# The chunk products of an RWKV-7 recurrence: 96 for 128, with operands laid side by side and over both partition halves

## The chip, the core and the metric

The kernel runs on one core of a Trainium2 chip. The metric is the device time of one execution in microseconds (us). Before the change it is 1353.78 us, the median of three runs from 1351.94 to 1355.68 us. All values are fp32.

## What is computed

One decoder layer over 1024 tokens of width 1024. A projection feeds two groups of heads, RWKV-7 (8 heads of 64) and latent attention (8 heads); their outputs are projected, added and normalised, and a feed-forward net of width 4096 follows. The change lies in the RWKV-7 recurrence, which the reference states token by token, for each head with a 64 x 64 state S:

```python
def step(S, inp):
    r_t, w_t, k_t, v_t, kk_t, a_t = inp
    sa = einsum('bhvk,bhk->bhv', S, -kk_t)
    S = S * w_t + sa (x) (kk_t * a_t) + v_t (x) k_t      # (x): outer product
    y = einsum('bhvk,bhk->bhv', S, r_t)
```

## The kernel before, in words

The recurrence (`rwkv_chunks`, L1603 to L1978) doesn't go token by token. It takes 16 chunks of 64 tokens, and in each chunk does the work of all eight heads with matrix products of 64 x 64. Heads are laid out as four tiles (`RT` = 4, loop variable c) of 128 partitions, and each tile holds two heads, one on partitions 0 to 63 and one on 64 to 127 (loop variable p, `own[p]`). A product of one head is so one matmul with 64 rows and 64 columns of TensorE, and the two heads of a tile stand at different places of the array. In the trace each fp32 matmul is two LDWEIGHTS and two MATMUL instructions; a tile shape such as 64*128 is rows * columns of the stationary operand in the array. "A pair" below is two MATMUL instructions, one for p = 0 and one for p = 1, that run side by side; the fp32 matmuls of both heads of a tile are two pairs.

PE's order is written out by hand in `stage(m, ...)` (L1803). Stage m does the chain of chunk n = m - 1 and prepares chunk m:

- `first_product(m)` (L1798): `low_t` times `inv`, 8 matmuls into bank `B_T1`
- `rhs_step(n)` (L1697): 16 matmuls, masked key scores times values, plus `kk` times state
- `scores_step(m)` (L1749): 24 matmuls. Three products of one form, decayed key with `kk` (A), decayed key with decayed receptance (R), and beta with decayed receptance
- `sa_step(n)` (L1713): 8 matmuls, the solve, into `B_SA`; ScalarE copies it to `u` (L1853)
- `product(B_X, ...)` (L1819): 8 matmuls, the second half of the chunk inverse; VectorE merges it (L1914)
- `transposes(m)` (L1767): 24 matmuls. Beta, decayed key and values, each times an identity or the centring matrix
- `state_step(n)` (L1722): 16 matmuls, two terms summed, key tokens times values and beta tokens times `u`
- `y_step(n)` (L1735): 24 matmuls, three terms summed

That makes 128 matmuls, or 256 MATMUL instructions, in a stage. Stages 1 to 15 do both halves; stage 16 has the chain alone, and before stage 1 chunk 0 is prepared.

ScalarE goes in the fixed order `product_out` (L1847), two exponentials (L1840, L1841), `u_step`, `tokens_step` (L1863 values, L1864 beta and key), `y_leave` (L1857). VectorE goes `rhs_out` (L1900), `mask_step` (L1923, L1925), `merged` (L1914), `state_out` (L1904, L1908), `r_step` (L1893). GpSimd makes the decayed key (L1977). SyncE's queue loads three 64 x 64 operands a head for chunk m, six DMAs (L1685), and for m >= 3 first waits for the solve of chunk m - 3 (L1678).

Of the kernel before, what the change touches and what calls it, by code (L numbers as in the profile page):

```python
# [24 lines left out]
P = 128  # L25
# [9 lines left out]
RT = RW // P  # L35
# [1567 lines left out]
def rwkv_chunks(nc, mem, k):  # L1603
# [26 lines left out]
    kd = [k.first_kd, new("k_undecayed", tile)]  # L1630
    rd = [k.first_rd] + new("r_decayed", tile, copies=2)
    ks = new("k_scores", [P, RT, 2, CH], copies=2)
    bs = new("b_scores", tile, copies=2)
    inv_t, inv, low_t = ([first] + new(name, tile, copies=2)
                         for first, name in zip(k.first_tiles, ("inverse_t", "inverse", "low_t")))
    bk_tok = new("bk_tok", [P, 2, RT, CH], copies=2)
    v_tok = new("v_tok", tile, copies=2)
    u = new("u", tile)
# [9 lines left out]
    B, K, A_, R = 0, 1, 0, 1  # L1648
    B_SA, B_RY, B_T1, B_X, B_KS, B_B, B_BKT, B_V = range(8)
    Y0 = RT  # L1650
    cols = lambda c: slice(c * CH, (c + 1) * CH)
    view = lambda bank, n=RT, at=0: ps[:, bank, at * CH:(at + n) * CH].rearrange("p (c n) -> p c n", n=CH)
    now = lambda m: slice(m * CH, (m + 1) * CH)

    with ExitStack() as ctx:
        exps, kd_ready, rd_ready, scores_mm, tr_done, sc_ready, tok_ready = sems(
            nc, ctx, "d_exps", "d_kd_ready", "d_rd_ready", "d_scores_mm", "d_tr_done", "d_sc_ready", "d_tok_ready")
# [11 lines left out]
        def _(sp):  # L1669
# [6 lines left out]
            for m in range(1, NC_):  # L1676
# [6 lines left out]
                for x, dst in ((k.inv_t_d, inv_t), (k.inv_d, inv), (k.low_d, low_t)):  # L1683
                    for p in range(2):
                        sp.dma_start(dst[m % 3][own[p], :, :], matrices(x)[:, m, p].rearrange("c r j -> r c j"))\  # L1685
                            .then_inc(base_in[m % 3], 16)
            sp.wait_ge(gate_in, 16)
# [6 lines left out]
        def _(pe):  # L1694
            mm = nc.tensor.matmul

            def rhs_step(n):  # L1697
                q, a = n % 2, n % 3
                pe.wait_ge(sc_ready, n + 1)
                pe.wait_ge(v_ready, n + 1)  # L1700
# [3 lines left out]
                for c in range(RT):  # L1704
                    for p in range(2):
                        mm(ps[own[p], B_RY, cols(c)], ks[q][own[p], c, A_, :], v_tok[q][own[p], c, :],
                           start=True, stop=False)
# [5 lines left out]
            def sa_step(n):  # L1713
                pe.wait_ge(rhs_ready, n + 1)
                pe.wait_ge(xt_up, n + 1)
                for c in range(RT):
                    for p in range(2):
                        last = mm(ps[own[p], B_SA, cols(c)], inv_t[n % 3][own[p], c, :], rhs[own[p], c, :],
                                  start=True, stop=True)
                last.then_inc(sa_mm, 1)  # L1720

            def state_step(n):  # L1722
                q = n % 2
                pe.wait_ge(tok_ready, n + 1)
                pe.wait_ge(sa_ready, n + 1)
                for c in range(RT):
                    for p in range(2):
                        mm(ps[own[p], B_SA, cols(c)], bk_tok[q][own[p], K, c, :], v_tok[q][own[p], c, :],
                           start=True, stop=False)
                    for p in range(2):  # L1730
                        last = mm(ps[own[p], B_SA, cols(c)], bk_tok[q][own[p], B, c, :], u[own[p], c, :],
                                  start=False, stop=True)
                last.then_inc(s_mm, 1)

            def y_step(n):  # L1735
                q, a = n % 2, n % 3
                for c in range(RT):
# [11 lines left out]
            def scores_step(m):  # L1749
                q, a = m % 2, m % 3  # L1750
                if m >= 1:
                    pe.wait_ge(kd_ready, m)
                    pe.wait_ge(rd_ready, m)
                    pe.wait_ge(sc_ready, m)
                for c in range(RT):
                    for p in range(2):
                        mm(ps[own[p], B_KS, cols(2 * c + A_)], kd[q][own[p], c, :], kk_all[own[p], c, now(m)],
                           start=True, stop=True)
                    for p in range(2):
                        mm(ps[own[p], B_KS, cols(2 * c + R)], kd[q][own[p], c, :], rd[a][own[p], c, :],  # L1760
                           start=True, stop=True)
                    for p in range(2):
                        last = mm(ps[own[p], B_B, cols(c)], beta[own[p], c, now(m)], rd[a][own[p], c, :],
                                  start=True, stop=True)
                last.then_inc(scores_mm, 1)

            def transposes(m):  # L1767
# [6 lines left out]
                for c in range(RT):  # L1774
                    for p in range(2):
                        mm(ps[own[p], B_BKT, cols(B * RT + c)], beta[own[p], c, now(m)], k.eye[own[p], :],
                           start=True, stop=True)
                    for p in range(2):
                        mm(ps[own[p], B_BKT, cols(K * RT + c)], kd[q][own[p], c, :], k.eye[own[p], :],
                           start=True, stop=True)  # L1780
                if m == 0:
                    pe.wait_ge(centred, 1)
                if m == 1 or m and m % 4 == 0:
                    pe.wait_ge(v_in[m // 4], 16)
                for c in range(RT):
                    for p in range(2):
                        v = hT[own[p], T_V + c, now(m)] if m else k.first_v[own[p], c, :]
                        last = mm(ps[own[p], B_V, cols(c)], v, centre[own[p], :], start=True, stop=True)
# [9 lines left out]
            def first_product(m):  # L1798
                z = m % 3
                pe.wait_ge(base_in[z], 96 * (m // 3 + (z > 0)))  # L1800
                product(B_T1, low_t[z], inv[z]).then_inc(t1_mm, 1)

            def stage(m, chain, ahead):  # L1803
# [11 lines left out]
                if ahead:  # L1815
# [3 lines left out]
                    product(B_X, prod, inv_t[z]).then_inc(xt_mm, 1)  # L1819
# [6 lines left out]
            product(B_T1, low_t[0], inv[0]).then_inc(t1_mm, 1)  # L1826
# [6 lines left out]
        def _(act):  # L1833
# [9 lines left out]
            def product_out(n):  # L1843
# [3 lines left out]
                A(prod[:], view(B_T1), ACT.Copy).then_inc(t1_out, 1)  # L1847

            def u_step(n):
                act.wait_ge(sa_mm, n + 1)  # L1850
                if n >= 1:
                    act.wait_ge(y_mm, n)
                A(u[:], view(B_SA), ACT.Copy).then_inc(sa_ready, 1)  # L1853
# [5 lines left out]
            def tokens_step(m):  # L1859
# [3 lines left out]
                A(v_tok[m % 2][:], view(B_V), ACT.Copy).then_inc(v_ready, 1)  # L1863
# [1378 lines left out]
```

## Time and profile before

| | |
|---|---|
| median of three runs | 1353.78 us |
| profiled execution, own time | 1353.33 us |
| its span | 1351.5 us |
| PE (TensorE) busy | 1315.0 us, 97% |
| VectorE busy | 945.5 us, 70% |
| ScalarE busy | 474.8 us, 35% |
| GpSimd busy | 497.0 us, 37% |
| TensorE clock granted | 0.998 of full speed (mean) |
| recurrence | from 475 to 605 us of the span, about a tenth |

A busy PE is not PE at its peak: matmuls are pipelined and overlap in the records, so what the recurrence costs is read from the times between the starts of instructions and not from their durations.

### The profile page before, as it was taken

What the parts mean: (1) busy time and instruction counts of PE and PEld (TensorE: products, weight loads), DVE (VectorE), ACT (ScalarE), POOL (GpSimd) and SP (SyncE); (2) the same over time, 40 slices, a digit from 0 to 9 for tenths busy, and PEclk for the clock granted to TensorE, in tenths of its full rate; (3) what the DMA queues carried; (4) which work ended last, traced back from release to release, by engine and by line L of the source; (5) the groups of instructions that cost most, each with busy time, mean ns of one, the idle gap of its engine ahead of it and who ended that gap; (6) DMA issues with size and microseconds to landing.
All of it is one profiled execution on the core that took longest, in us unless ns stands there. A gap on an engine that the chain in (4) does not pass through costs nothing.

```text
span 1351.5 us, 23894 instructions
## 1 busy us (share of the span) xinstructions
PE 1315.0 (97%) x9900; PEld 1071.2 (79%) x9900; DVE 945.5 (70%) x1110; ACT 474.8 (35%) x796; POOL 497.0 (37%) x323
## 2 busy tenths in 40 slices
PE   7999999999999989989999999999999999999997
PEld 6877677877776789986688878888888888888886
DVE  3657975257777634439677988877777787669877
ACT  3143643146555433334104522212222444333330
POOL 0000112001876210002084778766774354444030
PEclk9999999999999999999999999999999999999999
DMA  5111444779639952224222345444436986666562
GB/s 225 62 48 32 141 157 156 184 169 292 183 101 288 221 127 53 59 64 140 87 101 94 117 137 198 142 147 164 156 125 226 356 288 219 190 198 200 190 205 106
DMA packets 147372, 214.50 MB, mean 159 GB/s; under 512 B 79960, under 2 KB 86240, under 8 KB 146624
## 3 DMA queue, kind: packets, MB, share of 16 engines
q1 hardware_dynamic: 146976, 211.92, 49.3%
q8 instruction: 79, 1.29, 0.4%
q10 hardware_dynamic: 288, 1.05, 0.2%
q14 instruction: 29, 0.24, 0.1%
HBM read 137.89 MB, written 66.39 MB: 151 GB/s over the span
## 4 chain that ended last, share of the span: by engine, by line
PE 49%; DVE 3%; POOL 1%; issue 1%; ACT 1%; DVEq 0%; POOLq 0%; ACTq 0%
PE banks L2523 23%; PE banks L2410 18%; PE banks L2326 5%; PE banks L2398 2%; POOL tile_h L3083 1%; PE banks L2371 1%; DVE wout_lo L2736 0%; POOL tile_s L3083 0%; DVE y_all L2756 0%; DVE first_relu L2870 0%; PE banks L2352 0%; DVE gn_scale L2747 0%; PE banks L156 0%; PE banks L2337 0%; DVE yr_full L2762 0%
## 5 line engine op out<-in xcount | busy, mean ns | idle before, releaser
L2523 PE MATMUL banks<-stage_b_hi,stage_a_hi 128*128 128x512 f32 x448 | 174.3, 389 | 0.0
L2523 PE MATMUL banks<-stage_b_lo,stage_a_hi 128*128 128x512 f32 x448 | 174.3, 389 | 0.0
L2523 PE MATMUL banks<-stage_b_hi,stage_a_lo 128*128 128x512 f32 x448 | 174.3, 389 | 0.0
L2898 DVE TENSOR_TENSOR stage_a_lo<-stage_a_raw,stage_a_hi 128x1024 fp32r<-128x1024 f32 x56 | 97.7, 1745 | 35.2 <-ACT stage_a_hi L2665 35.2
L2665 ACT ACTIVATE stage_a_hi<-stage_a_raw 128x1024 fp32r<-128x1024 f32 x56 | 59.4, 1061 | 120.9 <-DMA stage_b_raw<-in_w_ffn 98.4
L2523 PEld LDWEIGHTS banks<-stage_b_lo,stage_a_hi 128*128 128x128 f32 x448 | 84.1, 188 | 17.6
L2523 PEld LDWEIGHTS banks<-stage_b_hi,stage_a_hi 128*128 128x128 f32 x448 | 84.1, 188 | 17.4
L2523 PEld LDWEIGHTS banks<-stage_b_hi,stage_a_lo 128*128 128x128 f32 x448 | 84.1, 188 | 17.3
L852 POOL TENSOR_TENSOR hT<-hT,rate 128x1024 f32<-128x1024 f32 x4 | 13.5, 3370 | 210.1 <-DVE kk_tile L773 210.1
L428 PE MATMUL banks<-xT_hi,win_hi 128*128 128x512 f32 x288 | 90.6, 396 | 0.0
L428 PE MATMUL banks<-xT_lo,win_hi 128*128 128x512 f32 x288 | 88.8, 389 | 0.0
L428 PE MATMUL banks<-xT_hi,win_lo 128*128 128x512 f32 x288 | 88.7, 389 | 0.0
L1347 ACT ACTIVATE probs<-banks,neg_row_max 128x512 f32<-128x512 f32 (+1 forms) x96 | 55.3, 581 | 63.9 <-DVE neg_row_max L1442 38.9
L1439 DVE TENSOR_REDUCE row_max_parts<-banks 128x1 f32<-128x512 f32 (+1 forms) x96 | 50.6, 552 | 33.1 <-PE banks L1212 17.8
L428 PEld LDWEIGHTS banks<-xT_hi,win_hi 128*128 128x128 f32 x288 | 53.1, 188 | 19.4 <-issue 8.2
L3107 POOL TENSOR_TENSOR w_slots<-stage_b_raw,w_slots 128x1024 f32<-128x1024 f32 x16 | 45.6, 2856 | 52.9 <-DMA stage_b_raw<-in_w_ffn 48.3
L428 PEld LDWEIGHTS banks<-xT_lo,win_hi 128*128 128x128 f32 x288 | 54.1, 188 | 11.4
L428 PEld LDWEIGHTS banks<-xT_hi,win_lo 128*128 128x128 f32 x288 | 54.1, 188 | 11.3
L2901 DVE TENSOR_TENSOR stage_b_lo<-stage_b_raw,stage_b_hi 128x1024 fp32r<-128x1024 f32 x34 | 53.5, 1574 | 0.4
L1225 PE MATMUL banks<-ident,probs 128*128 128x128 f32 x288 | 48.4, 287 | 4.6 <-ACT late_probs_t L1359 2.5
L1977 POOL TENSOR_TENSOR k_undecayed<-hT,undecay 128x256 f32<-128x256 f32 x15 | 11.1, 743 | 108.3 <-ACT undecay L1841 108.3
L2883 DVE SCALAR_TENSOR_TENSOR tile_h<-tile_h 128x512 f32<-128x512 f32 x56 | 47.6, 849 | 1.4
(423 smaller groups left out, 3590.1 us busy)
## 6 DMA issues: line engine op xcount, KB each, us to landing
stage_b_raw<-in_w_ffn SPq DMA_DIRECT2D x50, 512.0 KB, 5.0
stage_a_raw<-hid_s SPq DMA_DIRECT2D x32, 512.0 KB, 4.0
w_landed<-in_w_ffn SPq DMA_DIRECT2D x30, 512.0 KB, 4.7
hid_s<-tile_s SPq DMA_DIRECT2D x60, 256.0 KB, 4.4
stage_a_raw<-hid_h SPq DMA_DIRECT2D x24, 512.0 KB, 4.0
hid_h<-tile_h SPq DMA_DIRECT2D x42, 256.0 KB, 2.0
win_raw<-in_w_in SPq DMA_DIRECT2D x20, 512.0 KB, 3.6
x_tok<-in_x SPq DMA_DIRECT2D x8, 512.0 KB, 7.6
```

Source lines behind the costliest of these rows:

```text
L428: last = mm(ps[:, 2 * j + b, :], w[j][:, kt, :], r[:, kt, b * HALF:(b + 1) * HALF], start=kt == 0 and i == 0, stop=kt == KT - 1 and i == 2)
L1225: last = nc.tensor.transpose(ps[:, BANK_T + u % 2, j * P:(j + 1) * P], probs[n % 3][:, j * P:(j + 1) * P], ident[:])
L1347: A_(probs[n % 3][:, 0:width], ps[:, u % 4, 0:width], ACT.Exp, bias=bias[:, qt:qt + 1], scale=SCALE, accum_out=sums[:, m, qt:qt + 1]).then ...
L1439: step.mark(V.reduce_max(tops[:, m, qt:qt + 1], ps[:, u % 4, 0:blocks_of(i, u) * P], AX_X))
L2326: last = nc.tensor.matmul(ps[:, bank + b, :], a[:, kt % RT, tok], w[:, kt, b * HALF:(b + 1) * HALF], start=kt == W_ORDER[0] and n == 0, st ...
L2410: last = nc.tensor.matmul(ps[:, bank_of(u, name), :], a[:, j, cut], b(kt), start=kt == 0 and n == 0, stop=kt == HK - 1 and n == 2)
L2523: last = nc.tensor.matmul(ps[:, bank, :], s[a][:, j, tok], s[b][:, j, :], start=p == 0 and j == 0 and n == 0, stop=p == NP - 1 and j == 1 ...
L2665: A(s["a_hi"][:], s["a_raw"][:], COPY).then_inc(hi2, 1)
L2883: V.scalar_tensor_tensor(hid[name][:], hid[name][:], 0.0, hid[name][:], ALU.max, ALU.mult).then_inc(hid_done, 1)
L2898: V.tensor_tensor(s["a_lo"][:], s["a_raw"][:], s["a_hi"][:].bitcast(F32), ALU.subtract).then_inc(lo2, 1)
L2901: V.tensor_tensor(s["b_lo"][:], src, s["b_hi"][:].bitcast(F32), ALU.subtract).then_inc(lo2, 1)
L3107: G.tensor_tensor(dst, a, b, ALU.subtract).then_inc(combined, 1)
```

## The change

Seven things are changed, all in `rwkv_chunks`.

1. A new tile `bkb` holds beta, decayed key, beta side by side for each head: `[P, RT, 3, CH]`. GpSimd writes the decayed key into its middle. Beta comes by two new DMAs a chunk from SyncE's queue, one for each partition half, left of the key for one half of the heads and right of it for the other.
2. In `scores_step` the products R and beta become one matmul with 64 rows and 128 columns (`bkb[..., 1 - p:3 - p, :]`), whose result lies over all 128 partitions, in one bank for each p. Product A stays 64*64.
3. In `transposes` key and beta become one matmul of that shape too. The values stay 64*64.
4. `vu` holds values on one partition half and `u` on the other. `sa_step` writes the other half's partitions for this. `state_step` is then one matmul with 128 rows and 64 columns for two, and in `y_step` the values' and `u`'s terms become one of 128*64; the state's term stays 64*64.
5. ScalarE's copies of `u` and of the values become two of 64 partitions each. `u_step` no longer waits for `y_mm`.
6. VectorE's two mask operations swap size: first `ka` (128x256), then `rb` (128x512).
7. Banks are shared anew: A lies in the bank of the second product, values in that of the first. So `product(B_XA, ...)` waits for `ka_ready`, `scores_step` for `xt_up`, `first_product` for `v_ready`; and `scores_step` waits for `beta_in`.

Chunk 0 keeps 64*64 for its scores and transposes. Of the diff the core:

```diff
+    bkb = new("beta_k_beta", [P, RT, 3, CH], copies=2)
+    rb = new("y_scores", [P, 2, RT, CH], copies=2)
+    kb_tok = new("kb_tok", [P, 2, RT, CH], copies=2)
+    vu = new("vu", [P, 2, RT, CH], copies=2)
...
+                if m >= 3:
+                    sp.wait_ge(tr_done, m - 1)
+                for p in range(2):
+                    sp.dma_start(bkb[m % 2][own[p], :, 2 - 2 * p, :], beta[own[p], :, now(m)])\
+                        .then_inc(beta_in[m % 2], 16)
...
-                        last = mm(ps[own[p], B_SA, cols(c)], inv_t[n % 3][own[p], c, :], rhs[own[p], c, :],
+                        last = mm(ps[other[p], B_SA, cols(c)], inv_t[n % 3][own[p], c, :], rhs[own[p], c, :],
                                   start=True, stop=True)
...
 def state_step(n):
                 for c in range(RT):
                     for p in range(2):
-                        mm(ps[own[p], B_SA, cols(c)], bk_tok[q][own[p], K, c, :], v_tok[q][own[p], c, :],
-                           start=True, stop=False)
-                    for p in range(2):
-                        last = mm(ps[own[p], B_SA, cols(c)], bk_tok[q][own[p], B, c, :], u[own[p], c, :],
-                                  start=False, stop=True)
+                        last = mm(ps[own[p], B_SA, cols(c)], kb_tok[q][:, p, c, :], vu[q][:, p, c, :],
+                                  start=True, stop=True)
 def y_step(n):
                 for c in range(RT):
                     for p in range(2):
                         mm(ps[own[p], B_RY, cols(Y0 + c)], state[q][own[p], c, :], rd[a][own[p], c, :],
                            start=True, stop=False)
                     for p in range(2):
-                        mm(ps[own[p], B_RY, cols(Y0 + c)], v_tok[q][own[p], c, :], ks[q][own[p], c, R, :],
-                           start=False, stop=False)
-                    for p in range(2):
-                        last = mm(ps[own[p], B_RY, cols(Y0 + c)], u[own[p], c, :], bs[q][own[p], c, :],
+                        last = mm(ps[own[p], B_RY, cols(Y0 + c)], vu[q][:, p, c, :], rb[q][:, p, c, :],
                                   start=False, stop=True)
 def scores_step(m):                 # product A as before, then
+                        rd_now = rd[a][own[p], c, :]
+                        if m:
+                            last = mm(ps[:, B_RB + p, cols(c)], bkb[q][own[p], c, 1 - p:3 - p, :], rd_now,
+                                      start=True, stop=True)
 def transposes(m):
+                        if m:
+                            mm(ps[:, B_KB + p, cols(c)], bkb[q][own[p], c, 1 - p:3 - p, :], k.eye[own[p], :],
+                               start=True, stop=True)
 def first_product(m):
+                pe.wait_ge(v_ready, 2 * m)
 def stage(m, chain, ahead):
-                    product(B_X, prod, inv_t[z]).then_inc(xt_mm, 1)
+                    pe.wait_ge(ka_ready, m + 1)
+                    product(B_XA, prod, inv_t[z]).then_inc(xt_mm, 1)
 def u_step(n):
-                A(u[:], view(B_SA), ACT.Copy).then_inc(sa_ready, 1)
+                for p in range(2):
+                    A(vu[n % 2][other[p], p, :, :], ps[other[p], B_SA, 0:RT * CH].rearrange("p (c n) -> p c n", n=CH),
+                      ACT.Copy).then_inc(sa_ready, 1)
```

## Rows read from the trace of the kernel before

**Rows 1.** Windows, the recurrence: us, busy us of each engine (instructions), clock, DMA share.

```profile
475.00:604.00 129.00, 120.90 (x3947) 117.88 (x3948) 52.28 (x120) 40.25 (x107) 11.11 (x15) 1.00 0.31 76
```

**Rows 2.** Waits in 475 to 604 us: total us, times, longest.

```profile
ACT u L1853 <- PE banks L1718: 35.7, 16, 2.7
```

**Rows 3.** Timeline, one stage: start us, us from first start to last end, engine, instructions.

```profile
540.09 0.31 PE L1728 MATMUL banks<-v_tok,bk_tok 64*64 64x64 f32 x4
...
542.42 0.66 PE L1794 MATMUL banks<-inverse,low_t 64*64 64x64 f32 x16
...
542.65 0.38 ACT L1857 ACTIVATE y_all<-banks 128x256 f32<-128x256 f32 x1 [1.46 <-PE banks L1745]
...
543.15 0.22 PEld L1706 LDWEIGHTS banks<-v_tok,k_scores 64*64 64x64 f32 x4 [0.21 <-issue]
...
544.13 0.31 PE L1757 MATMUL banks<-kk_all,k_undecayed 64*64 64x64 f32 x4
...
545.53 0.66 PE L1718 MATMUL banks<-rhs,inverse_t 64*64 64x64 f32 x16
...
545.77 0.69 DVE L1923 TENSOR_TENSOR k_scores<-banks,mask 128x512 f32<-128x512 f32 x1 [0.97 <-PE banks L1763]
...
547.87 0.31 PE L1728 MATMUL banks<-v_tok,bk_tok 64*64 64x64 f32 x4
```

**Rows 4.** One line each: durations ns min/median/max, first and last start.

```profile
L1757 PE MATMUL banks<-kk_all,k_undecayed x256: 218/218/267, 471.4 to 593.5; 64*64 64x64 f32 x128
...
L1925 DVE TENSOR_TENSOR b_scores<-banks,mask x16: 411/414/416, 473.7 to 594.5; 128x256 f32<-128x256 f32 x16
...
L1853 ACT ACTIVATE u<-banks x16: 384/384/387, 479.2 to 601.8; 128x256 f32<-128x256 f32 x16
```

**Rows 5.** Timeline of PE and PEld around L466, shape 64*128.

```profile
130.21 1.99 PE L466 MATMUL banks<-hT,w_lora 64*128 64x512 f32 x8
...
130.74 1.02 PE L466 MATMUL banks<-hT,w_lora 64*128 64x512 f32 x4
...
131.17 1.02 PE L466 MATMUL banks<-hT,w_lora 64*128 64x512 f32 x4
...
132.13 0.73 PE L428 MATMUL banks<-xT_hi,win_hi 128*128 128x512 f32 x2
...
L466 PEld LDWEIGHTS banks<-hT,w_lora x32: 182/186/187, 130.2 to 214.5; 64*128 64x128 f32 x32
...
130.21 0.30 PEld L466 LDWEIGHTS banks<-hT,w_lora 64*128 64x128 f32 x4 [0.35 <-issue]
```

**Rows 6.** Timeline of PE around L1251, shape 128*64.

```profile
319.08 1.95 PE L1251 MATMUL banks<-late_probs_t,v_all 128*64 128x256 f32 x16
...
319.35 0.82 PE L1251 MATMUL banks<-late_probs_t,v_all 128*64 128x256 f32 x6
...
319.57 0.82 PE L1251 MATMUL banks<-late_probs_t,v_all 128*64 128x256 f32 x6
...
320.96 0.55 PE L1225 MATMUL banks<-ident,probs 128*128 128x128 f32 x3
```

**Rows 7.** Timeline of PE into and out of the 64*64 products of L485.

```profile
172.11 0.56 PE L485 MATMUL banks<-kk_tile,beta_tile 64*64 64x64 f32 x12
...
173.62 0.57 PE L485 MATMUL banks<-kk_tile,beta_tile 64*64 64x64 f32 x14
...
174.12 1.13 PE L156 MATMUL banks<-key_norms,head_rows 32*128 32x512 f32 x4
```

**Rows 8.** SyncE's queue and PE early in the recurrence, and landing (KB, us).

```profile
474.96 1.28 SPq L1685 DMA_DIRECT2D low_t<-low_d  x2
...
477.05 0.33 PE L1757 MATMUL banks<-kk_all,k_undecayed 64*64 64x64 f32 x4 [0.94 <-POOL k_undecayed L1977]
...
low_t<-low_d SPq DMA_DIRECT2D x30, 64.0 KB, 3.0
```

More of the change, by code:

```diff
@@ L1752, in scores_step @@
                     pe.wait_ge(kd_ready, m)
+                    pe.wait_ge(beta_in[q], 32 * ((m + 1) // 2))
                     pe.wait_ge(rd_ready, m)
-                    pe.wait_ge(sc_ready, m)
+                    pe.wait_ge(rb_ready, m)
+                    pe.wait_ge(xt_up, m)
                 for c in range(RT):
                     for p in range(2):
-                        mm(ps[own[p], B_KS, cols(2 * c + A_)], kd[q][own[p], c, :], kk_all[own[p], c, now(m)],
-                           start=True, stop=True)
+                        kd = bkb[q][own[p], c, 1, :] if m else k.first_kd[own[p], c, :]
+                        mm(ps[own[p], B_XA, cols(A0 + c)], kd, kk_all[own[p], c, now(m)], start=True, stop=True)
                     for p in range(2):
[L1760 to L1764, printed above, removed]
+                        rd_now = rd[a][own[p], c, :]
+                        if m:
+                            last = mm(ps[:, B_RB + p, cols(c)], bkb[q][own[p], c, 1 - p:3 - p, :], rd_now,
+                                      start=True, stop=True)
+                        else:
+                            mm(ps[own[p], B_RB + p, cols(c)], k.first_kd[own[p], c, :], rd_now, start=True, stop=True)
+                            last = mm(ps[other[p], B_RB + p, cols(c)], beta[own[p], c, now(0)], rd_now,
+                                      start=True, stop=True)
                 last.then_inc(scores_mm, 1)
@@ L1775, in transposes @@
                     for p in range(2):
[L1776 to L1780, printed above, removed]
+                        if m:
+                            mm(ps[:, B_KB + p, cols(c)], bkb[q][own[p], c, 1 - p:3 - p, :], k.eye[own[p], :],
+                               start=True, stop=True)
+                        else:
+                            mm(ps[own[p], B_KB + p, cols(c)], k.first_kd[own[p], c, :], k.eye[own[p], :],
+                               start=True, stop=True)
+                            mm(ps[other[p], B_KB + p, cols(c)], beta[own[p], c, now(0)], k.eye[own[p], :],
+                               start=True, stop=True)
                 if m == 0:
                     pe.wait_ge(centred, 1)
+                    pe.wait_ge(t1_out, 1)
                 if m == 1 or m and m % 4 == 0:
@@ L1787, in transposes @@
                         v = hT[own[p], T_V + c, now(m)] if m else k.first_v[own[p], c, :]
[L1788 removed]
+                        last = mm(ps[own[p], B_TV, cols(V0 + c)], v, centre[own[p], :], start=True, stop=True)
                 last.then_inc(tr_done, 1)
@@ L1800, in first_product @@
                 pe.wait_ge(base_in[z], 96 * (m // 3 + (z > 0)))
-                product(B_T1, low_t[z], inv[z]).then_inc(t1_mm, 1)
+                pe.wait_ge(v_ready, 2 * m)
+                product(B_TV, low_t[z], inv[z]).then_inc(t1_mm, 1)
             def stage(m, chain, ahead):
@@ L1824, in stage @@
                     y_step(n)
-            product(B_T1, low_t[0], inv[0]).then_inc(t1_mm, 1)
+            product(B_TV, low_t[0], inv[0]).then_inc(t1_mm, 1)
             scores_step(0)
```

62 lines of the change are left out of this document (32 added, 30 removed).

## The prediction, made before the changed kernel ran

> **What bounds the recurrence now.** I read the page's busy shares first, then the recurrence as one window, its waits, and last one stage in order of time. The window has TensorE at 120.9 of 129 us, with the clock granted in full [rows 1]. The others wait for PE; the longest wait that counts is ScalarE's for the solve, 35.7 us [rows 2]. A stage lasts 547.87 - 540.09 = 7.78 us [rows 3]. The 24 pairs of the scores take 545.53 - 544.13 = 1.40 us, 58.3 ns a pair, and 128 pairs make 7.46 us. The rest, 0.3 us, is one gap: `rhs_step` waits for ScalarE's copy of y, which ends at 543.03, and loads at 543.15 [rows 3]. So the stage is a stream of PE instructions and nearly nothing else, and the sum goes by intervals between starts. Where one step of the stage follows another (at 545.53, say), each with semaphores to pass, nothing is lost.
>
> **What one pair costs in each shape.** Before, all is 64*64. After, a stage has three shapes.
> - 128*64 (state, y): the trace has it at L1251 with 256 moving columns. Its pairs start 0.22 us apart (319.35, 319.57) where one of them streams 0.38 [rows 6], so the two column halves do run side by side, and the load of the next pair is hidden. With 64 moving columns I take the 58 ns of 64*64.
> - 64*128 (R with beta, key with beta): at L466 the pairs start 0.43 us apart, and both row halves run side by side. But four weight loads, two pairs, take 0.30 us with 0.186 for one, so a pair of loads of 128 columns takes 0.107 us or so [rows 5]. With only 64 columns to stream, the load sets the interval: 0.11 us. Bounds: 0.058 (the load costs nothing more) and 0.19 (no overlap at all). This halves the count of instructions and saves 5%: two 64*64 pairs were 0.117.
>
> TensorE: Matmul & The Clock Gate, a page of the Trainium skill, says in Packing small matmuls that a weight load overlaps matmuls in flight only where its row group differs. In 128*64 all tiles share their rows, and each load would then stand exposed: by it `state_step` would be some 0.4 us longer and the total about 6 us higher. The hidden loads at L1251 speak against it, and I don't take it.
>
> **What a change of shape costs.** This the trace shows at each border between shapes.
> - Leaving: the last 64*64 pair of L485 starts at 173.62 + 0.57 - 0.218 = 173.97 and the next shape at 174.12, 0.15 us for 0.058 [rows 4, 7]. From 128*64 it is 320.96 - (319.08 + 1.95 - 0.38) = 0.31 for 0.22 [rows 6]; from 64*128, 132.13 - (130.21 + 1.99 - 0.59) = 0.52 for 0.43 [rows 5]. It is some 0.09 us each time.
> - Entering: the first interval is longer by one load. 64*128: 0.53 for 0.43 (130.21, 130.74) [rows 5]. 64 columns: L485's twelve instructions last 0.56, with 0.218 for the last and four intervals of 0.058, which leaves 0.11 for the first [rows 7]; at L1251 it is 0.27 for 0.22 [rows 6]. With short streams: 0.11 us for 64 columns, two loads or 0.21 for 128.
>
> So one change costs 0.14 to 0.19 us, the price of two or three pairs. A stage after has 20: into and out of 64*128 for each of four tiles in the scores (8), into it and out of it in the transposes (2), into 128*64 for the state (1), twice for each tile in y (8), and out at the end (1). Before it has none.
>
> That 64*64 to 64*128 is a change as well, no row shows: rows 5 to 7 all have a border where the rows, or the columns from 128, change. L1251's border changes columns alone, and that is nearest, so I count it in full. TensorEngine Tiling (Array Packing), in the Trainium skill under Key Properties, says that changing the tiling mode drains TensorE while changing only the tile does not, and lists 64*64 and 64*128 as different modes; by it the sum stands, without it the second rival holds.
>
> **A stage after**, in us, from the intervals above (a group of two pairs that is entered and left is 0.11 + 0.15 = 0.26, in 64*128 0.21 + 0.15 = 0.36):
> - rhs, 16 pairs: 0.93
> - scores: product A 0.06 + 0.15, then 3 x 0.26; R with beta 4 x 0.36: 2.45 (before 1.40)
> - solve, entered: 0.11 + 7 x 0.058 = 0.52 (0.47)
> - the new wait for `ka`: 0.18
> - second product, left: 7 x 0.058 + 0.15 = 0.56 (0.47)
> - key with beta: 0.21 + 6 x 0.11 + 0.15 = 1.02, values 0.11 + 6 x 0.058 + 0.15 = 0.61 (together 1.40)
> - state: 0.61 (0.93)
> - y: 8 x 0.26 = 2.08 (1.40)
> - first product, entered: 0.52 (0.47), and the wait for y's copy: 0.16 (0.3)
>
> Sum 9.64, against 7.78: +1.86, and x 15 stages +27.9 us. Two terms need their working. VectorE starts the mask 0.30 us after the last pair of the scores (545.77 - 545.47), `ka` takes 0.41 like `b_scores` [rows 3, 4], and PE goes on 0.12 after such an end (543.03 to 543.15): 0.84 us in all. PE would be there after 0.15 + 0.52 = 0.67 or so, hence 0.18; queued behind it are the transposes, state and y, all of PE. Bounds 0 and 0.4. Y's copy frees the right-hand sides 0.8 us after the last pair of y (542.36 to 543.15); leaving and entering now fill 0.14 of that, which is a gain.
>
> **Once each.** Stage 16: state -0.32, y +0.68, and ScalarE's second copy of `u`, +0.38 for a 64-partition copy taken like one of 128 [rows 4]; +0.7. In the other stages the second product and the transposes hide that copy. Stage 1: the first two beta DMAs stand in SyncE's queue behind the six loads for chunk 1, of which the last, `low_t`, is issued by 474.96 + 1.28 = 476.24 [rows 8]. At 0.64 us an issue the second of them goes at 476.9 and lands 3.0 later like the others of 64 KB, at 479.9, while the scores start at 477.05: +2.9 us (bounds 0 and 4). Later ones have a stage of lead. Eight issues of 0.65 us fit a stage, so SyncE's queue holds. The rest costs nothing: VectorE's masks have the same sum, GpSimd's 11.11 / 15 = 0.74 us a stage [rows 1] only gets a stride, `first_product`'s wait for the values' copies and `scores_step`'s for the merge fall on things done 2 us before. ScalarE gets 0.77 us more a stage in which it worked 31% of the time [rows 1]. The layer outside is untouched.
>
> 27.9 + 0.7 + 2.9 = 31.5 us. The profiled execution took 1353.3, within 0.5 of the median, and makes 1384.8; I say 1385.
>
> **Rivals.**
> 1. *Changes of shape are dear, but 64*64 with 64*128 shares its row halves and is none.* Ten changes stay. Scores 1.34, solve and product 0.93, the wait 0.31 as PE comes sooner, key with beta 0.88, values 0.56, the rest as above: 8.3 a stage, +0.53. With the single terms 11.6 us: 1365. For it: no row. Against: L1251's border.
> 2. *Changes cost nothing in the recurrence* (the price seen at borders would be that of a long stream ending), and the change saves. 64 + 16 pairs at 0.058 and 16 at 0.11, the wait 0.31, the gap 0.3: 7.0 a stage, -0.77, -11.5 in all, last chunk -0.6, first DMA +2.9: 1344. If loads of 128 columns were free too, 12 less: 1332. This is the other side, and it decides at a price of some 0.04 us a change. Against it: L485 has 64 moving columns like the recurrence, and pays.
> 3. *Short bursts pay more*, 0.05 us a change on top, as each load waits for the drain and nothing is queued deep enough behind: 20 x 0.05 x 15 = +15: 1400.
>
> **Chances.** Forecast 0.68, first rival 0.10, second 0.12, third 0.10. The range 1362 to 1398 takes in the forecast with its bounds (the waits give -6 to +5, a load of 0.19 us rather than 0.11 in 14 unentered pairs a stage +17, which I hold unlikely), the first rival and half of the third. About 0.3% (4 us) can be told from no change: faster 0.12, the same 0.03, slower 0.85.
>
> **What would show it.** In the profile after, a stage of 9.6 us; starts 0.15 us apart at each border of shapes, and 0.26 for each group in y; the 64*128 loads 0.11 apart within the key transposes; fewer MATMULs yet PE still the one that is waited for; in stage 1 a gap of 3 us before the scores. It is wrong if a stage is under 7.8 us, if the border between the A products and the R products has no gap, or if the waits for `ka` or beta recur in each stage with more than 0.4 us.

## The result, and the profile after

The changed kernel takes 1391.66 us (median of 4 runs, 1388.43 to 1392.45) against 1352.86 (median of 4, 1350.97 to 1355.68). The ratio is 1.0281, with its 95% interval 1.026 to 1.0303: slower, by 38.8 us, where 31.5 were forecast. The profiled execution is the fastest of the four, 1388.43 us with a span of 1386.6, and is read against the 1351.5 of before: +35.1.

The page's busy row and its clock row (40 slices, tenths of full speed):

```profile
PE 1351.3 (97%) x8908; PEld 1085.0 (78%) x8908; DVE 943.9 (68%) x1110; ACT 488.1 (35%) x828; POOL 496.9 (36%) x323
...
PEclk9999999999999889999999999999999999999999
```

PE has 8908 MATMULs for 9900, a tenth less in the whole kernel, and is busy for 36 us longer, at the same share of 97%. The clock row has two slices of 8, where the recurrence begins; before has 9 in all forty.

One stage of the kernel after, PE in order of time (start, us from first start to last end, line, tile, instructions), answers to [rows 3]:

```profile
564.35 0.33 PE L1715 MATMUL banks<-vu,k_scores 64*64 64x64 f32 x4
...
565.30 0.31 PE L1764 MATMUL banks<-kk_all,beta_k_beta 64*64 64x64 f32 x4
565.54 0.44 PE L1768 MATMUL banks<-r_decayed,beta_k_beta 64*128 64x64 f32 x4
565.91 0.33 PE L1764 MATMUL banks<-kk_all,beta_k_beta 64*64 64x64 f32 x4
...
567.80 0.68 PE L1727 MATMUL banks<-rhs,inverse_t 64*64 64x64 f32 x16
568.49 0.68 PE L1807 MATMUL banks<-inverse_t,product 64*64 64x64 f32 x16
569.10 1.11 PE L1786 MATMUL banks<-eye,beta_k_beta 64*128 64x64 f32 x16
570.14 0.68 PE L1801 MATMUL banks<-centre,hT 64*64 64x64 f32 x16
570.75 0.69 PE L1737 MATMUL banks<-vu,kb_tok 128*64 128x64 f32 x16
571.37 0.33 PE L1746 MATMUL banks<-r_decayed,state 64*64 64x64 f32 x4
571.63 0.34 PE L1749 MATMUL banks<-y_scores,vu 128*64 128x64 f32 x4
...
573.47 0.68 PE L1807 MATMUL banks<-inverse,low_t 64*64 64x64 f32 x16
574.12 0.33 PE L1715 MATMUL banks<-vu,k_scores 64*64 64x64 f32 x4
```

It lasts 574.12 - 564.35 = 9.77 us, and all of stages 3 to 15 do, against 7.78. Each term of the forecast is a difference of two starts (y: to 573.47, the last group's start is 573.21):

| part | forecast | measured |
|---|---|---|
| rhs | 0.93 | 0.95 |
| scores | 2.45 | 2.50 |
| solve and the wait for `ka` | 0.70 | 0.69 |
| second product | 0.56 | 0.61 |
| key with beta | 1.02 | 1.04 |
| values | 0.61 | 0.61 |
| state | 0.61 | 0.62 |
| y | 2.08 | 2.10 |
| first product and y's copy | 0.68 | 0.65 |
| stage | 9.64 | 9.77 |

Group by group the reader sees the price of a change of shape. A products to R products, 565.54 - 565.30 = 0.24 (forecast 0.21, as the first A group is left but not entered); an R group, entered and left, 565.91 - 565.54 = 0.37 (forecast 0.36). The later A groups, entered too, take 0.26, as forecast. In y every group of two pairs is 0.26, where 64*64 pairs in a row take 0.117 for two. No "idle before" stands in any of these rows: PE counts as busy through all of it.

What the steady stage doesn't tell is stage 1. Its wait, and SyncE's queue ahead of it, which answer to [rows 8]:

```profile
479.48 0.48 PE L1764 MATMUL banks<-kk_all,beta_k_beta 64*64 64x64 f32 x4 [4.44 <-DMA beta_k_beta<-beta_all]
```

```profile
474.08 2.48 SPq L1687 DMA_DIRECT2D low_t<-low_d  x2
476.61 1.28 SPq L1692 DMA_DIRECT2D beta_k_beta<-beta_all  x2
```

The windows over stages 1 and 2 (length, busy us of PE, PEld, DVE, ACT, POOL with instructions, then the granted clock, the DMA share and GB/s):

```profile
470.00:480.00 10.00, 4.70 (x166) 4.37 (x166) 3.29 (x8) 3.55 (x9) 1.65 (x2) 0.83 0.46 115
480.00:490.00 10.00, 9.35 (x110) 7.98 (x112) 1.47 (x3) 1.06 (x4) 0.00 (x0) 0.50 0.60 166
490.00:500.00 10.00, 10.00 (x144) 8.30 (x144) 2.08 (x6) 2.69 (x7) 0.72 (x1) 0.65 0.50 120
500.00:510.00 10.00, 9.98 (x200) 8.40 (x198) 3.30 (x8) 3.58 (x10) 0.72 (x1) 1.00 0.25 54
```

PE waits 4.44 us for the beta DMA, and the clock falls to 0.50, the lower of its two levels (1.2 for 2.4 GHz), from 476.6 to 497.1 us. PE is recorded as busy 9.35 and 10.00 of 10 us in most of that stretch. Two rows of it:

```profile
490.90 0.48 PE L1746 MATMUL banks<-r_decayed,state 64*64 64x64 f32 x4
491.31 0.48 PE L1749 MATMUL banks<-y_scores,vu 128*64 128x64 f32 x4
```

A group of y takes 0.41 us here for the 0.26 at the full clock, 1.6 times as long at half the clock. Before, PE waited 0.94 us at the same place [rows 8], and the clock was full throughout the recurrence [rows 1].

The account of the +35.1 us: 15 stages x 1.99 = +29.9; stages 1 and 2 beyond that +7.9 (31.8 now, 19.9 before); stages 3 to 15 of before are together 3.4 us longer than 13 x 7.78, mostly behind idle times of 0.56, 0.20 and 1.23 us that the profile puts to "issue" (PE waited for nothing that it shows), and those of after have no such excess: -3.4; the last chunk and what follows +1.7; and the recurrence begins 1.1 us earlier, -1.1. Sum +35.0. The last term has nothing to do with the change: the code ahead of the recurrence is the same, and the profile of before has 3.4 us of low clock there (from 430 us) that the one of after doesn't have.

### The profile page after: what moved, and what is told of

It reads as the page before. It is cut to its first block, busy times and chain, and to the rows that moved or that the text cites. A ratio compares the mean times of both kernels' runs of the same rounds, so it can differ in the third digit from the quotient of the medians.

```text
span 1386.6 us, 21990 instructions
## 1 busy us (share of the span) xinstructions
PE 1351.3 (97%) x8908; PEld 1085.0 (78%) x8908; DVE 943.9 (68%) x1110; ACT 488.1 (35%) x828; POOL 496.9 (36%) x323
## 4 chain that ended last, share of the span: by engine, by line
PE 49%; DVE 3%; POOL 1%; issue 1%; ACT 0%; DVEq 0%; POOLq 0%; ACTq 0%
PE banks L2541 22%; PE banks L2428 17%; PE banks L2344 5%; PE banks L2416 2%; PE banks L2355 1%; POOL tile_h L3101 1%; PE banks L2389 1%; POOL tile_s L3101 0%; DVE y_all L2774 0%; DVE first_relu L2888 0%; DVE wout_lo L2754 0%; PE banks L2370 0%; DVE gn_scale L2765 0%; PE banks L156 0%; DVE yr_full L2780 0%
## 5 line engine op out<-in xcount | busy, mean ns | idle before, releaser
L2916 DVE TENSOR_TENSOR stage_a_lo<-stage_a_raw,stage_a_hi 128x1024 fp32r<-128x1024 f32 x56 | 104.4, 1864 | 37.6 <-ACT stage_a_hi L2683 37.6
L2541 PEld LDWEIGHTS banks<-stage_b_hi,stage_a_hi 128*128 128x128 f32 x448 | 84.1, 188 | 17.6
L2541 PEld LDWEIGHTS banks<-stage_b_hi,stage_a_lo 128*128 128x128 f32 x448 | 84.1, 188 | 17.3
L1995 POOL TENSOR_TENSOR beta_k_beta<-hT,undecay 128x256 f32<-128x256 f32 x15 | 11.1, 740 | 140.2 <-ACT undecay L1856 140.2
```

Source lines behind the costliest of these rows:

```text
L2541: last = nc.tensor.matmul(ps[:, bank, :], s[a][:, j, tok], s[b][:, j, :], start=p == 0 and j == 0 and n == 0, stop=p == NP - 1 and j == 1 ...
L2916: V.tensor_tensor(s["a_lo"][:], s["a_raw"][:], s["a_hi"][:].bitcast(F32), ALU.subtract).then_inc(lo2, 1)
```

## The experiments

Two theories stood at the start. **A**: the price is that of changing TensorE's tile shape, 0.14 us each, 20 times a stage, plus stage 1, where the wait for beta also costs the clock. **B**: the price lies in the new shapes themselves (a 64*128 or 128*64 product is slow among short ones, however they are ordered), and the low clock follows from them. The kernel before, measured beside the variants, has medians of 1355.46 to 1355.61 us, some 2.7 us above the 1352.86 beside the change, so a difference of medians between the change and a variant is good to about 3 us.

### Fewer changes of shape, the same products

`e2_grouped`: the 8 A products first and then the 8 wide ones; in y all 128*64 products first (straight behind the state's, of the same shape), then the state's term. 6 changes a stage for 20, with the same 96 products.

```diff
                         mm(ps[own[p], B_XA, cols(A0 + c)], kd, kk_all[own[p], c, now(m)], start=True, stop=True)
+                for c in range(RT):
                     for p in range(2):
...
+                for c in range(RT):
+                    for p in range(2):
+                        mm(ps[own[p], B_RY, cols(Y0 + c)], vu[q][:, p, c, :], rb[q][:, p, c, :],
+                           start=c == 0, stop=False)
+                for c in range(RT):
+                    for p in range(2):
+                        last = mm(ps[own[p], B_RY, cols(Y0 + c)], state[q][own[p], c, :], rd[a][own[p], c, :],
+                                  start=False, stop=c == RT - 1)
```

> The changed kernel, with the same products in another order: in the scores all A products, then all R with beta; in y all 128*64 products (right behind the state's, of the same shape), then all state products. 96 products as before, 6 changes of shape a stage for 20. Theory (each border between shapes costs 0.14 to 0.19 us): a steady stage falls from 9.77 to about 7.7 us, the kernel by 31 us to about 1361. Rival (the gaps come of products that add into one region right behind one another, or of both partition halves of a bank being written): these stay, the stage stays above 9 us and the kernel above 1380.

Measured: 1356.06 us (10 runs), ratio 1.001 (0.9998 to 1.0021). One stage of it, PE:

```profile
562.95 0.33 PE L1715 MATMUL banks<-vu,k_scores 64*64 64x64 f32 x4
...
563.90 0.66 PE L1765 MATMUL banks<-kk_all,beta_k_beta 64*64 64x64 f32 x16
564.49 1.11 PE L1770 MATMUL banks<-r_decayed,beta_k_beta 64*128 64x64 f32 x16
565.53 0.68 PE L1727 MATMUL banks<-rhs,inverse_t 64*64 64x64 f32 x16
...
568.48 0.69 PE L1737 MATMUL banks<-vu,kb_tok 128*64 128x64 f32 x16
568.99 0.64 PE L1746 MATMUL banks<-y_scores,vu 128*64 128x64 f32 x16
569.56 0.68 PE L1750 MATMUL banks<-r_decayed,state 64*64 64x64 f32 x16
570.08 0.63 PE L1809 MATMUL banks<-inverse,low_t 64*64 64x64 f32 x16
570.82 0.33 PE L1715 MATMUL banks<-vu,k_scores 64*64 64x64 f32 x4
```

The stage is 570.82 - 562.95 = 7.87 us. Fourteen changes less save 9.77 - 7.87 = 1.90 us, 0.136 us each, in place of the 0.14 to 0.19 of the forecast. Counted where they fall, the six fewer in the scores save 2.50 - (565.53 - 563.90) = 0.87, 0.145 each, and the eight fewer of state and y 2.72 - (570.08 - 568.48) = 1.12, 0.14 each; the first product and the wait for y's copy take 0.09 of it back (0.74 for 0.65). In the scores no product adds into the place of another, so the rival of that kind falls there too. The other six at that price are 0.82, and without them 7.05 would be left, the 7.0 of the second rival. So theory B falls for the steady stage: in their new shapes the products run at the prices forecast, 0.058 us a pair of 128*64 and 0.11 one of 64*128, and what they save is about 0.73 us a stage; the changes cost 2.7. The kernel gained more than the 31 us expected: its profile is 32.4 us shorter, 28.5 of them 15 x 1.90, and most of the rest lies in stages 1 and 2, where the low stretch is shorter.

### The clock: wait or order

`e1_beta_first` issues chunk 1's two beta DMAs ahead of all other loads of the recurrence.

```diff
+            betas(1)
             values(0)
             for m in range(1, NC_):
...
+                if m > 1:
+                    betas(m)
```

> The changed kernel, with the two beta DMAs of chunk 1 issued first in SyncE's queue. Theory: PE's wait of 4.4 us for them in stage 1 (474.8 to 479.5) both stands in the way and drops the TensorE clock to its lower level, from 476.6 to 497.1 us, which stretches stages 1 and 2. Then the clock stays at 1.00 there, stage 1 falls from 21.2 us to about 11, stage 2 from 10.6 to 9.8, and the kernel is 11 us faster than the changed one, about 1380. Rival: the clock falls because stages of stacked shapes keep the array too little at work at the start, whatever the wait; then the low stretch is still there, and only about 3 us go, to 1388.

Measured: 1381.22 us (4 runs, 1378.49 to 1384.85), ratio 1.0203 (1.0175 to 1.0231): some 10 us better than the change. PE in stage 1, then the window:

```profile
474.14 0.50 PE L1813 MATMUL banks<-inverse_t,product 64*64 64x64 f32 x9 [1.11 <-issue]
...
476.18 0.40 PE L1770 MATMUL banks<-kk_all,beta_k_beta 64*64 64x64 f32 x4 [0.61 <-POOL beta_k_beta L2001]
```

```profile
476.00:494.00 18.00, 17.17 (x218) 14.53 (x218) 3.32 (x8) 3.75 (x10) 1.27 (x2) 0.53 0.70 178
```

The wait for beta is gone, but the clock still fell in this execution, from 476.3 to 493.4, behind a halt of 1.11 us and a wait of 0.61. Stage 1 is 17.3 us for 21.2, not the 11 expected, and the two profiles are only 4.7 us apart; the rest of the 10 us is that the change's other three executions ran at mean clocks of 0.983 to 0.985 and these at 0.992 to 0.998. Half a miss for theory A: without the wait the clock may stay (a run at a mean clock of 0.998 took 1378.49, the profiled one at 0.992 took 1383.67), but it needn't.

`e4_before_wait` puts the wait alone into the kernel before: the same two DMAs into a tile that nobody reads, and PE waits for them in stage 1.

```diff
+                if m == 1:
+                    for p in range(2):
+                        sp.dma_start(spare[own[p], :, :], beta[own[p], :, now(m)]).then_inc(beta_in, 16)
...
+                    if m == 1:
+                        pe.wait_ge(beta_in, 32)
```

> The kernel before, with two DMAs of beta for chunk 1 into a spare tile, behind the loads of chunk 1 in SyncE's queue, and PE's wait for them ahead of the scores of stage 1. Theory: a wait of 3 to 4 us more, and the clock falls to its lower level also in this kernel, whose products are all 64*64; stage 1 goes from 10.1 us to 16 or more, and the kernel is 8 us slower or more, 1361. Rival (the low clock belongs to the stacked shapes): the clock stays 1.00, only the wait is added, 1356.

Measured: 1360.02 us (9 runs), ratio 1.0039 (1.0025 to 1.0054). Its gap and its windows:

```profile
479.70 0.33 PE L1765 MATMUL banks<-kk_all,k_undecayed 64*64 64x64 f32 x4 [3.54 <-DMA spare<-beta_all]
```

```profile
480.00:484.00 4.00, 3.80 (x77) 3.61 (x73) 1.02 (x2) 0.55 (x2) 0.00 (x0) 0.57 0.39 88
484.00:500.00 16.00, 14.99 (x482) 14.50 (x484) 5.12 (x12) 5.10 (x14) 1.45 (x2) 1.00 0.63 167
```

A gap of nearly the same length has the low clock behind it among 64*64 products as well, but for 3.4 us (480.3 to 483.7) and not for 20.5. So the low clock doesn't need the new shapes. In size the theory missed: stage 1 is 14.3 us, not 16 or more, and the kernel 4.5 us slower, not 8; and of what it lost, a part lies elsewhere, for at 595 us PE halts for another 2.88 us ("issue"), with 3.4 us of low clock behind it.

That the wait takes the clock fits, and isn't shown by one profile: ahead of the recurrence every kernel here waits 2.05 to 2.14 us at one and the same place (L1260 of before), and behind it five profiles (before, `e2_grouped`, `e3_scores64`, `e5_y_grouped_64`, `e9_solve_values`) have 3.4 us of low clock, the other six none.

`e6_grouped_beta_first` is `e2_grouped` with `betas(1)` first.

> e2 (grouped, 6 changes of shape, 64*128 scores and transposes, stage 7.87) with the beta DMAs of chunk 1 first, as in e1. Theory A (the wait for beta and the low clock behind it both go once PE is also busier in its stages): 1356 - 7 = 1349, clock 1.00 from 470 to 510. Theory B (as e1 showed: the clock falls there without that wait too, and lasts as long as PE's stages are loose): the low stretch is there but shorter than e1's 17 us, only 3 us go, 1353.

Measured: 1352.76 us (10 runs), ratio 0.9978 (0.9966 to 0.9991). PE in stage 1, and the windows:

```profile
474.37 0.33 PE L1721 MATMUL banks<-vu,k_scores 64*64 64x64 f32 x4 [0.45 <-issue]
...
476.59 0.68 PE L1771 MATMUL banks<-kk_all,beta_k_beta 64*64 64x64 f32 x16 [1.07 <-POOL beta_k_beta L2003]
```

```profile
470.00:480.00 10.00, 7.18 (x225) 6.55 (x224) 4.31 (x10) 4.30 (x11) 1.65 (x2) 1.00 0.48 116
480.00:490.00 10.00, 9.28 (x226) 8.52 (x224) 3.52 (x8) 3.87 (x10) 0.72 (x1) 1.00 0.72 206
```

The clock never falls in the recurrence, though the wait of 1.07 us is longer than that of 0.61 in `e1_beta_first`; stage 1 is 10.9 us for the 17.3 of `e2_grouped`. So theory A is right on this profile, but the time is that of theory B, 1353 and not 1349. Two reasons show: with beta first, stage 2 waits 1.17 us for `low_t` (9.3 us for 7.9), and the ten executions have mean clocks from 0.994 to 0.999, so some of them may have lost the clock. In `e2_grouped` the low stretch was 13.6 us (behind a gap of 3.97), in `e1_beta_first` 17.1, in the change 20.5. That fewer changes of shape behind the gap bring the clock back sooner fits these three, but they are single profiles.

### Which of the new shapes pays

`e3_scores64` keeps the stacked state and y products (8 saved) and gives up key beside beta: the scores and transposes are 64*64 in every chunk, with no beta DMA. 112 products, 10 changes.

```diff
-                            last = mm(ps[:, B_RB + p, cols(c)], bkb[q][own[p], c, 1 - p:3 - p, :], rd_now,
-                                      start=True, stop=True)
+                        kd = bkb[q][own[p], c, 1, :] if m else k.first_kd[own[p], c, :]
+                        mm(ps[own[p], B_RB + p, cols(c)], kd, rd_now, start=True, stop=True)
+                    for p in range(2):
+                        last = mm(ps[other[p], B_RB + p, cols(c)], beta[own[p], c, now(m)], rd[a][own[p], c, :],
+                                  start=True, stop=True)
```

> The changed kernel, with scores and transposes back in 64*64 products for every chunk (R and beta each by itself, no beta DMA, no beta_in wait); only state and y are stacked: 112 products. 10 changes of shape a stage. Theory: scores 1.40, key and beta 0.93, state 0.61, y 2.08, a stage of about 8.4 us for 9.77, and no wait in stage 1, so 1391 - 20 - 11 = about 1361. Rival (64*64 to 64*128 costs nothing and the loss lies in 128*64 alone): the stage stays above 9.3 us.

Measured: 1356.48 us (10 runs, 1351.66 to 1360.46), ratio 1.0009 (0.9991 to 1.0026). The stage is 7.63 us, a miss against the 8.4 expected. The first rows of its scores, and the start of the solve behind them:

```profile
523.74 0.25 PE L1756 MATMUL banks<-kk_all,beta_k_beta 64*64 64x64 f32 x2
523.78 0.27 PE L1762 MATMUL banks<-r_decayed,beta_all 64*64 64x64 f32 x2
523.80 0.25 PE L1756 MATMUL banks<-kk_all,beta_k_beta 64*64 64x64 f32 x2
523.86 0.22 PE L1760 MATMUL banks<-r_decayed,beta_k_beta 64*64 64x64 f32 x1
...
523.98 0.25 PE L1756 MATMUL banks<-kk_all,beta_k_beta 64*64 64x64 f32 x2
```

...and 24 rows further on:

```profile
524.65 0.22 PE L1720 MATMUL banks<-rhs,inverse_t 64*64 64x64 f32 x1
```

Three lines run interleaved, and 24 products take 524.65 - 523.74 = 0.91 us for the 1.40 of before. The key products write the partition half that they read, the beta products the other one; the two kinds use different quarters of the array, and four products go side by side and not two: 0.91 us is what the 16 key products take alone, two by two (0.93), so those of beta ride along free. The expectation had them at two by two, and so missed. In stage 2 this kernel loses it again: PE halts 3.08 us for no reason that the profile shows, and the clock is at 0.50 for 10.2 us behind it. The ten executions go with it: 1351.66 and 1351.84 us at mean clocks of 0.999 and 0.997, 1359.83 and 1360.46 at 0.989.

```profile
491.74 0.37 PE L1776 MATMUL banks<-eye,beta_k_beta 64*64 64x64 f32 x2 [3.08 <-issue]
```

`e7_beta_apart` tests that reading: all beta products behind all key products (one more `for c in range(RT):` ahead of them), the same instructions.

> e3 with the same products in another order: in scores and transposes the beta products of all tiles come after all products of the key, where e3 has them side by side for each tile. Theory (in e3 the products into the own half and those into the other half run four at a time, in different quarters of the array, so its 24 score products took 0.91 us for 1.40): here only two run at a time, scores 1.40, key and beta 0.93, a stage of about 8.4 us for 7.63, the kernel 12 us slower than e3, 1368. Rival (e3 is fast for another reason, such as the banks): no change.

Measured: 1359.05 us (10 runs), ratio 1.0024 (1.0011 to 1.0037), stage 8.03 us. Its scores:

```profile
544.87 0.31 PE L1756 MATMUL banks<-kk_all,beta_k_beta 64*64 64x64 f32 x4
544.99 0.31 PE L1760 MATMUL banks<-r_decayed,beta_k_beta 64*64 64x64 f32 x4
...
546.13 0.63 PE L1720 MATMUL banks<-rhs,inverse_t 64*64 64x64 f32 x16
```

The scores take 546.13 - 544.87 = 1.26 us: the key products alone go at two by two again (0.117 a group), and only where beta meets the last of them do four overlap. The reading holds; the size was missed, as that overlap was not foreseen: a stage is 0.40 us longer and not 0.8, which makes 6 us over 15 stages, not 12. The median is 2.6 us above that of `e3_scores64`; what narrows it further is that the profile of that one has the 3-us halt and 10 us at the low clock, which this one lacks in those stages.

### Both together, and what then stands in the way

`e5_y_grouped_64` is `e3_scores64` with y grouped as in `e2_grouped`: 112 products, 2 changes a stage.

> Scores and transposes in 64*64 as in the run before (e3, a steady stage of 7.63 us), and in y all 128*64 products behind the state's, then all state products: 112 products, 2 changes of shape a stage. Theory (0.14 us a change of shape; R, key on one hand and beta on the other run four at a time in the four quarters of the array): state and y together go from 0.61 + 2.10 to 1.08 + 0.52, first product and gap from 0.67 to 0.76, a stage to about 6.6 us, so 15 us under e3: about 1341, 1% faster than the kernel before. Rival (with so little on PE, ScalarE and the wait for ka hold the stage): 7.2 us and no less, 1350.

Measured: 1345.61 us (6 runs), ratio 0.9927 (0.9911 to 0.9943). The best stages are 6.61 us as expected (6.6), but only some are. Of the rest, PE's waits of 480 to 600 us put 9.8 us to "issue" (total us, times, longest); two of six such rows:

```profile
PE banks L1777 <- issue: 3.3, 2, 2.8
PE banks L1743 <- issue: 2.9, 2, 2.7
```

They sum to 9.8 us, against 3.5 before and none after the change. Behind the two longest the clock is low for 3.4 us each.

`e8_y_grouped_spread` spreads SyncE's loads of the later values and of the gate, all issued in stage 3, over stages 3 to 11, on the idea that the halts come from a crowded DMA queue.

```diff
-                if m == 3:
-                    for n in range(1, 4):
-                        values(n)
-                    sp.dma_start(k.gate[:], k.later).then_inc(gate_in, 16)
+                if m in (3, 6, 9):
+                    values(m // 3)
+                if m == 11:
+                    sp.dma_start(k.gate[:], k.later).then_inc(gate_in, 16)
```

> e5 with the loads of values 1 to 3 and of the gate spread over the loop (at chunks 3, 6, 9 and 11 and not all at chunk 3). Theory: the halts of 1.4 to 3.3 us in the middle of PE's stream, for which no releaser is shown, are fetches of its instructions that stand behind those four large loads (DMA share 0.83 at 480 to 490 us in e3), and the clock falls behind them; then the halt near 488 us goes and e8 is 3 to 8 us faster than e5. Rival: the halts have nothing to do with these loads, no change within 2 us.

Measured: 1344.36 us (5 runs), ratio 0.9915 (0.9898 to 0.9932), not told apart from the last, as its rival said. The halt of 2.77 us near 491 us and the low clock behind it are gone, but others came: they sum to 11.8 us, the largest row being

```profile
PE banks L1743 <- issue: 4.6, 2, 3.0
```

`e9_solve_values` adds the four quarters to the solve: its products (which write the other half) and the values' transposes (which write their own) alternate.

```diff
+                    if beside:
+                        for p in range(2):
+                            mm(ps[own[p], B_TV, cols(V0 + c)], hT[own[p], T_V + c, now(m)], centre[own[p], :],
+                               start=True, stop=True)
                     for p in range(2):
                         last = mm(ps[other[p], B_SA, cols(c)], inv_t[n % 3][own[p], c, :], rhs[own[p], c, :],
                                   start=True, stop=True)
```

> e8 (112 products, all scores and transposes 64*64, y grouped, loads spread) with the solve and the transposes of the values side by side, tile by tile: the solve goes from the own into the other half of the array, the values stay in their own half, so the four quarters should work at once. Theory (four at a time): the values' 0.47 us go out of the stage, 6.6 to about 6.15 us, the kernel 5 to 7 us faster than e8, 1338. Rival (the wait for ka behind the scores, 0.45 us in e8's stage, only grows, since the solve was what filled it): no gain, 1344.

Measured: 1342.79 us (5 runs), ratio 0.9906 (0.9888 to 0.9924). The solve, the values beside it, and the next product:

```profile
522.91 0.22 PE L1727 MATMUL banks<-centre,hT 64*64 64x64 f32 x1
522.96 0.22 PE L1730 MATMUL banks<-rhs,inverse_t 64*64 64x64 f32 x1
...
523.82 0.62 PE L1808 MATMUL banks<-inverse_t,product 64*64 64x64 f32 x14 [0.18 <-DVE k_scores L1942]
```

The 16 products of both take less than 0.6 us for 0.93, but the best stages are 6.49 us and not 6.15, since the product behind them now waits for VectorE's `ka` (its rival, in part), and over all stages halts sum to 11.6 us. It is 1.6 us better than the last and not told apart from it; of all versions it is the fastest, 0.9% under the kernel before.

## Why the prediction was right, and where its size was off

- **PE bounds, and its intervals give the sum**: right. All nine rows of the stage are within 0.05 us; 9.77 for 9.64. Three slips in its working change next to nothing: the terms of the scores add up to 2.43 and not 2.45; 0.30 - 0.186 in [rows 5] is 0.114 and not 0.107; and if 64*64 to 64*128 were no change, the first rival would hold and not the second.
- **A change of shape costs 0.14 to 0.19 us**: right, 0.14 by the comparison of 20 with 6 (0.136 with what a later wait took back). That 64*64 to 64*128 is a change, which no row of before showed, is right too: 0.24 at 565.30 for a group that takes 0.117 among its like. The first rival (10 changes free, 8.3 a stage) falls by that row; the second (all free) falls at once, though its 7.0 us is what the products alone cost. The rule of the Trainium skill (TensorEngine Tiling (Array Packing), Key Properties) that changing the mode drains TensorE agrees with these rows, in both directions and for both new shapes. The third rival's extra 0.05 us for short bursts isn't there: 0.13 a stage is the whole excess.
- **Loads in 128*64 are hidden**: right. The state's 8 pairs take 0.62 us, entered, at the 58 ns forecast. The other rule of the Trainium skill (TensorE: Matmul & The Clock Gate, Packing small matmuls), by which a load overlaps only where its row group differs and would be exposed here, is contradicted by this row.
- **A 64*128 pair is bound by its loads, 0.11 us**: right; key with beta is 1.04 for 1.02, and within it loads start 0.11 apart (569.32, 569.43, 569.54).
- **The wait for `ka`, 0.18**: right; 0.69 for the 0.70 of solve and wait. VectorE's `ka` ends at 568.34, and PE goes on at 568.49.
- **Once each, stage 1, +2.9 us**: this is the mis-sized term. Stages 1 and 2 cost 7.9 us beyond their new length. The wait itself is 4.44 us instead of 0.94 [rows 8], 3.5 more and not 2.9: the data is there 0.4 us earlier than forecast (479.5 for 479.9), though `low_t`'s issue took 2.48 us for 1.28, but PE comes 1.1 us earlier too. The rest is the clock, of which "Once each" said nothing. Of the 20.5 low microseconds 17.6 lie behind the gap, with PE at work. The two stages are 12.3 us longer than 2 x 9.77: 4.4 for the wait, and 7.9 for the low clock with a wait of 0.65 for ScalarE in it. Those of before were 4.3 us longer than 2 x 7.78, by waits and halts; the difference is the 7.9 of the account.
- **Stage 16, +0.7**: 1.7 with all that follows it, where the last y products and those of the next part ran at the low clock again, for 6.8 us.
- **What the forecast didn't have**: the 3.4 us of halts of before in stages 3 to 15, which are gone (after has 20 MATMULs a us where before has 33; that this is why isn't shown). +2.0 (stages), +5.0 (stage 1 and 2), +1.0 (end), -3.4 and -1.1 (start) is 3.5 of the 3.6 us by which the profile missed 31.5. That it is so little is in part luck: three terms were 8.0 us short, and 4.5 us that nobody had forecast, 1.1 of them chance, went the other way. The median is 3.2 above the profiled run, at mean clocks of 0.983 to 0.985 in the three other runs for 0.988.

Left open: what sets how long the clock stays low (more changes of shape behind the gap go with it in three profiles, but `e3_scores64`, with 10 changes a stage, had 10.2 us and a second time 3.4), why it falls behind a wait in one profile and not in another, and what the "issue" halts are. That they come where PE's stream is densest is seen; that they are instructions that arrive late is only an idea. And the plainest rival of the fastest versions wasn't run: the kernel before with nothing changed but beta's products, which would write the other partition half beside the key's. The best stage of `e5_y_grouped_64` is 1.17 us under 7.78. The quarters give 0.94 (0.49 in the scores, 0.45 in the transposes), stacking state and y gives 0.73 (1.60 for 2.33), and the solve with the wait for `ka` behind it takes 0.39 back (0.86 for 0.47). What the quarters alone would come to, and so what stacking adds, isn't known.

## What to carry to other kernels

Don't count matmuls, count changes of tile shape: in a stream of 58-ns pairs one costs as much as two or three of them, so a stacked or widened operand pays only if all products of its shape stand together (96 products: +38.8 us with 20 changes, nothing with 6). The version with 2 changes gains 10 us, but more of its saving comes from the quarters (0.94 us a stage) than from stacking (0.73). With 64*64 products, look first whether neighbours can write opposite partition halves, for then four go at once without any new shape. And a wait of some microseconds that a new load puts ahead of PE may take the clock along; price it with a range for that, not by its length alone.

## What the runs showed that was not expected

- Four 64*64 matmuls run side by side when their stationaries and outputs fall into the four quarters of the array and alternate in the stream: 24 products in 0.91 us, 16 transposes of key and beta in 0.48, for 1.40 and 0.93 two by two.
- The clock fell to its lower level behind idle times of PE of 4.44 us (the change), 3.97 (`e2_grouped`), 3.54 and 2.88 (`e4_before_wait`), 3.08 (`e3_scores64`), 2.97 (`e8_y_grouped_spread`), 2.77 and 2.69 (`e5_y_grouped_64`) and 1.96 (`e9_solve_values`), but also behind 1.11 and 0.61 us close together (`e1_beta_first`), 1.06 (`e3_scores64`, near its end) and 0.97 (the change and `e7_beta_apart`, in the last chunk). It stayed up behind 1.23 us before, 1.35 in `e7_beta_apart`, 1.62 in `e8_y_grouped_spread`, and behind the same 0.97 in the last chunk of other kernels. So the length of a wait didn't tell by itself. It was back after 3.4 us seven times (once with 10 changes of shape a stage, else with 0 or 2), and after 6.8 us at the end of the change and of `e7_beta_apart`; 10.2, 13.6, 17.1 and 20.5 us are one profile each, with 10, 6, 20 and 20 changes, with PE recorded as busy for most of the stretch.
- PE halts of 0.2 to 3.1 us with no releaser go with how many MATMULs a microsecond the steady stage has, not with its length. Their sums from 480 to 600 us: none at 20 (the change, `e1_beta_first`); 0 and 0.5 us at 24 (`e2_grouped`, `e6_grouped_beta_first`); 2.0 at 28 (`e7_beta_apart`) and 4.5 at 29 (`e3_scores64`); 3.5 and 4.7 at 33 (before, `e4_before_wait`); 9.8 to 11.8 at 34 and 35 (`e5_y_grouped_64`, `e8_y_grouped_spread`, `e9_solve_values`).
